# Sixteen instead of twelve pairs of projection tiles as block products, and the token-shift mixer's chunks refilled with six or seven tiles

## What is computed

```python
h = layer_norm(x)
u = h @ w_in                                   # 1024 x 14720: 115 tiles of 128 columns
u_gate, u_gla, u_rwkv, u_ssm = split(u)
o_gla  = gated_linear_attention(u_gla)         # chunked scan
o_rwkv = token_shift_mixer(u_rwkv)             # us = u + (u_previous - u) * mu, then a chunked scan
o_ssm  = ssd(silu(causal_conv(u_ssm)))         # four taps over time, then a chunked scan
merged = g0 * (o_gla @ gla_wo) + g1 * (o_rwkv @ rwkv_wo) + g2 * (o_ssm @ ssm_wo)
h = layer_norm(alpha * x + merged @ w_out)
h = layer_norm(alpha * h + moe(h))
```

## Time and profile before

| | us |
|---|---|
| median of 3 runs | 1493.3 (1489.31 to 1493.69) |
| the profiled execution | 1490.3 |
| its span | 1488.5 |
| PE busy | 1437.6 (97%) |
| DVE, ACT, POOL busy | 724.7 (49%), 418.2 (28%), 205.4 (14%) |

### The profile page before, as it was taken

How to read it: one execution, slowest core, us unless ns; L and a number is a source line. 1 busy time by engine, 2 the same in 40 slices (tenths; PEclk the granted TensorE clock), 3 DMA queues, 4 the chain that set the end, 5 groups by cost and what they waited for, 6 DMA issues and landing times.

```text
span 1488.5 us, 32593 instructions
## 1 busy us (share of the span) xinstructions
PE 1437.6 (97%) x13647; PEld 1051.5 (71%) x13647; DVE 724.7 (49%) x1345; ACT 418.2 (28%) x965; POOL 205.4 (14%) x171
## 2 busy tenths in 40 slices
PE   7999999999999999999999999999999999999995
PEld 6997666777776777777668986776575767676751
DVE  7445787875735777734547654522212121121228
ACT  2335434343223544435432211111111111111111
POOL 3771113122010000020022000000101000010000
PEclk9999999999999999999999999999999999999998
DMA  8888466363345444664576638599999999999984
GB/s 281 186 162 172 152 159 182 111 212 96 110 119 160 115 117 119 204 184 131 161 262 183 215 139 359 198 385 401 420 427 427 426 429 429 425 428 429 429 342 202
DMA packets 157042, 375.38 MB, mean 252 GB/s; under 512 B 101724, under 2 KB 110316, under 8 KB 139232
## 3 DMA queue, kind: packets, MB, share of 16 engines
q1 hardware_dynamic: 140928, 345.78, 65.8%
q0 software_dynamic: 6576, 16.48, 3.2%
q10 hardware_dynamic: 9392, 11.06, 2.2%
HBM read 327.14 MB, written 51.95 MB: 255 GB/s over the span
## 4 chain that ended last, share of the span: by engine, by line
PE 79%; DVE 9%; DMA 5%; DVEq 2%; issue 2%; ACT 1%; ACTq 1%; SPq 0%; POOLq 0%
PE PS L698 21%; PE PS L1250 14%; PE PS L1217 7%; PE PS L1269 6%; PE PS L1096 6%; PE PS L715 6%; DVE region L1730 4%; PE PS L780 3%; PE PS L1222 2%; PE PS L1138 2%; DVE region L1737 2%; DMA region<-projected 2%; PE PS L788 1%; PE PS L1233 1%; DMA region<-expert_rows 1%
## 5 line engine op out<-in xcount | busy, mean ns | idle before, releaser
L698 PE MATMUL PS<-h0T,region 128*128 128x320 f32 x1424 | 406.6, 438 | 1.0 <-issue 1.0
L1353 ACT ACTIVATE region<-PS 128x320 f32<-128x320 f32 (+7 forms) x408 | 154.5, 389 | 682.7 <-PE PS L698 233.1
L698 PEld LDWEIGHTS PS<-h0T,region 128*128 128x128 f32 x1424 | 264.0, 190 | 113.5 <-issue 12.1
L1250 PE MATMUL PS<-region 128*64 128x512 f32 x1024 | 228.8, 592 | 0.0
L1250 PEld LDWEIGHTS PS<-region 128*64 128x64 f32 x1024 | 124.4, 137 | 92.2 <-issue 32.0
L1730 DVE TENSOR_TENSOR region<-region 128x512 f32<-128x512 f32 (+10 forms) x230 | 154.3, 691 | 30.3 <-DMA region<-wo 6.5
L1353 ACT ACTIVATE region<-region 128x256 f32<-128x256 f32 (+11 forms) x229 | 99.4, 465 | 116.2 <-DVEq L2148 24.1
L1269 PE MATMUL PS<-region,history 128*64 128x512 f32 x512 | 119.7, 596 | 0.8 <-ACTq L1692 0.5
L1217 PEld LDWEIGHTS PS<-region,h 128*128 128x128 f32 x864 | 100.6, 192 | 22.3 <-issue 22.2
L1730 DVE TENSOR_TENSOR history<-region,PS 128x256 f32<-128x256 f32 x32 | 13.5, 421 | 196.5 <-ACTq L1687 196.4
L1217 PE MATMUL PS<-region,h 128*128 128x128 f32 x864 | 108.1, 278 | 0.3 <-issue 0.3
(11 more groups left out here) (239 smaller groups left out, 1594.8 us busy)
## 6 DMA issues: line engine op xcount, KB each, us to landing
region<-moe_w SPq DMA_DIRECT2D x64, 2048.0 KB, 17.9
region<-moe_w SPq DMA_DIRECT2D x64, 1024.0 KB, 15.6
region<-w_in SPq DMA_DIRECT2D x115, 512.0 KB, 5.7
region<-wo SPq DMA_DIRECT2D x32, 512.0 KB, 4.7
projected<-region ACTq DMA_DIRECT2D x64, 167.5 KB, 3.7
expert_rows<-region SPq DMA_DIRECT2D x20, 512.0 KB, 7.0
region<-expert_rows SPq DMA_DIRECT2D x5, 2048.0 KB, 15.2
region<-projected SPq DMA_DIRECT2D x10, 768.0 KB, 6.5
```

The costliest lines, as they stand in the source:

```text
L698: last = mm(PS[:, 6 + i % 2, 0:NTOK], WR[:, i, k, :], H0T[:, k, :], start=(k == 0), stop=(k == KT - 1))
L1250: last = mm(PS[tiles(i), 2, :], XE[:, k, tiles(i)], W13[r][i][:, k * 512:k * 512 + 512], start=(k == 0), stop=(k == KT - 1))
L1353: return nc.scalar.activation(out, in_, f, **kw)
```

## The change

**Order of the tiles.** `PRE` is 36: sixteen pairs are block products, and 32 tiles instead of 40 are left for the chunks. The list `FILLS` gives the chunks 6, 6, 6, 7 and 7 of them. A table `TILE` maps the place n to the feature: the 24 convolved features stand at the places `MIXED`, which are the first two tiles behind the pairs and the first four (chunks 0 to 2) or five (chunks 3 and 4) fills of each chunk. The four new pairs are `T_MISC` and tiles of the state-space gate. The first store of the mixer's last rows and their load are done at pair 11.

**Inside a chunk.** Round 1 is followed by half a tile (six fills) or a whole one (seven), round 2 by half a tile, round 3 by none, round 4 by half a tile, and where there are six fills the half tile behind round 5 is left out. DVE convolves behind round 0, behind round 2 (seven fills only), behind the `SAS` copy and twice behind the `YS` copy; the other places are gone.

**Other edits.** ACT copies the chunk edges and the history of a tile (two small ACTIVATEs) only where they are used. Counts of semaphores follow `PRE`. SP's code shown above has the same order as before; only the value waited for on `conv_stored` is written as a count over `MIXED`.

```diff
-PRE = 28
+PRE = 36
-HEAD_R, FILL = 4, 8
+HEAD_R = 4
+FILLS = (6, 6, 6, 7, 7)
+STARTS = [N_RW + sum(FILLS[:c]) for c in range(NCH)]
+MIXED = [PRE, PRE + 1, *(STARTS[c] + f for c in range(NCH) for f in range(4 if c < 3 else 5))]
+def mixed_until(n):
+    return sum(1 for m in MIXED if m < n and m % RING == n % RING)
...
             for i in range(RING):
-                sp.wait_ge(sem(f"conv_stored{i}"), 16 * (24 // RING))
+                sp.wait_ge(sem(f"conv_stored{i}"), 16 * mixed_until(NT + (i - NT) % RING))
...
@@ PE, rwkv
-                one = c + 1
+                one, seven, final = c + 1, FILLS[c] == 7, FILLS[c] - 1
-                    if r in (1, 2):
-                        fill(2 + r)
-                    if r == 3:
-                        fill(5, first)
+                    if r == 1:
+                        fill(3, range(KT) if seven else first)
+                    if r == 2:
+                        fill(4 if seven else 3, first if seven else second)
                     if r == 4:
-                        fill(5, second)
+                        fill(4, second if seven else first)
...
-                fill(6, first)
+                if seven:
+                    fill(5, first)
                 pe.wait_ge(sem("rw_tt"), one)
...
-                fill(6, second)
+                fill(5 if seven else 4, second)
...
@@ ACT, move and rwkv
-                a_(STG[:, i, 1:NPC, 0:HIST], src[:, 0:NPC - 1, L - HIST:L], ACT.Copy)
-                a_(STG[:, i, 0:NCH:NPC, 0:HIST], HISTS[:, n, :, :], ACT.Copy)
+                if mixed or n < T_MISC:
+                    a_(STG[:, i, 1:NPC, 0:HIST], src[:, 0:NPC - 1, L - HIST:L], ACT.Copy)
+                    a_(STG[:, i, 0:NCH:NPC, 0:HIST], HISTS[:, TILE[n], :, :], ACT.Copy)
...
-                    if r < 3:
-                        fill(2 + r)
+                    if r == 0:
+                        fill(2)
+                    if r == (1 if FILLS[c] == 7 else 2):
+                        fill(3)
...
@@ DVE, rwkv
                 if late:
-                    convolve(N_RW + c * FILL - 2)
                     late_variance(c - 1)
...
-                convolve(N_RW + c * FILL + 3)
+                convolve(STARTS[c] + (2 if FILLS[c] == 7 else 1))
...
-                for f in (4, 5):
-                    convolve(N_RW + c * FILL + f)
+                for f in (3, 4) if FILLS[c] == 7 else (2, 3):
+                    convolve(STARTS[c] + f)
```

More of the change, by code:

```diff
@@ L45 @@
 N_RW = PRE + HEAD_R
-N_S0 = N_RW + NCH * FILL
+STARTS = [N_RW + sum(FILLS[:c]) for c in range(NCH)]
+N_S0 = N_RW + sum(FILLS)
 N_SSM = N_S0 + HEAD_S
@@ L50, with _order @@
 assert N_GLA + NPC * FILL_G == NT and N_S0 >= T_GLA and N_G0 >= T_GATE
+FIRST_IN = 16 * (PRE // RING - PAIRS // 4)
+MIXED = [PRE, PRE + 1, *(STARTS[c] + f for c in range(NCH) for f in range(4 if c < 3 else 5))]
+assert len(MIXED) == T_Z - T_XBC
+def _order():
+    others = iter([*range(T_Z, NT)])
+    conv = iter(range(T_XBC, T_Z))
+    rw = [n if n < 16 else n + 8 if n < 18 else n - 2 for n in range(T_MISC)]
+    return [*rw, T_MISC, *(next(conv) if n in MIXED else next(others) for n in range(T_MISC + 1, NT))]
+TILE = _order()
+assert sorted(TILE) == list(range(NT)) and TILE[N_S0:] == list(range(N_S0, NT))
+def mixed_until(n):
+    return sum(1 for m in MIXED if m < n and m % RING == n % RING)
 V_MU, V_W0, V_A0, V_KK, V_KA, V_RK, V_LNG, V_LNB = 0, 26, 34, 42, 50, 58, 66, 74
@@ L452, in fill_weights @@
             def fill_weights(c, fs):
-                for f in fs:
-                    weights(c * (FILL // RING) + (N_RW + f) // RING, (N_RW + f) % RING)
+                for n in (STARTS[c] + f for f in fs):
+                    weights(n // RING, n % RING)
             def state_out(s):
@@ L470, in _ @@
                 chunk_rows(c + 1)
-                fill_weights(c, range(FILL))
+                fill_weights(c, range(FILLS[c]))
                 clear_rows(c)
@@ L474, in _ @@
             chunk_rows(NPC)
-            fill_weights(NPC - 1, range(FILL))
+            fill_weights(NPC - 1, range(FILLS[NPC - 1]))
             fill_weights(NPC, range(RING))
@@ L478, in _ @@
             sp.dma_start(SS, io['st_rwkv']).then_inc(sem("state_in"), 16)
-            fill_weights(NPC, range(RING, FILL))
+            fill_weights(NPC, range(RING, FILLS[NPC]))
             def conv_rows(c):
@@ L917, in rwkv @@
                     front_bonus(c + 1)
-                fill(7, range(KT) if ahead else first)
+                fill(final, range(KT) if ahead else first)
                 pe.wait_ge(sem("rw_copied"), c * 4 + 3)
@@ L923, in rwkv @@
                 else:
-                    fill(7, second)
+                    fill(final, second)
             for n in range(PRE, N_RW):
@@ L1383, in move @@
                 n = m * RING + i
-                mixed = isinstance(n, int) and T_XBC <= n < T_XBC + 24
+                mixed = n in MIXED
                 act.wait_ge(sem("tile_done"), n + 1)
@@ L1475, in fill @@
                 def fill(f):
-                    move(c * (FILL // RING) + (N_RW + f) // RING, (N_RW + f) % RING)
+                    n = STARTS[c] + f
+                    move(n // RING, n % RING)
                 one, w = c + 1, banks(0, 2, 8, 2, L)
@@ L1510, in rwkv @@
                     front_exp(c + 1)
-                fill(5)
-                fill(6)
-                for f in range(7, FILL):
+                for f in range(4, FILLS[c]):
                     fill(f)
@@ L1832, in quads @@
                 dve.wait_ge(sem("quad_kept"), 4 * p + 1)
+                for n in (RING + 2 * p, RING + 2 * p + 1):
+                    if n - RING >= T_MISC:
+                        dve.wait_ge(sem(f"store_done{n % RING}"), (n // RING + 1) * 16)
                 tt(quad_out(a, 0), kept(u, 0), Z, add)
@@ L1842, in paired_shift @@
             def paired_shift(n):
-                i, row = n % RING, head_row(n)
+                i, row = n % RING, TILE[n]
                 dve.wait_ge(sem("tile_moved"), n + 3)
@@ L1862, in convolve @@
             def convolve(n):
[L1864 to L1866 removed]
+                i, k = n % RING, TILE[n] - T_XBC
                 tap = lambda q: VEC[:, V_CW + 24 * q + k:V_CW + 24 * q + k + 1]
@@ L2024, in rwkv @@
                 dve.drain().then_inc(sem("rw_copied"), 1)
-            for n in range(PRE - 1, PRE + 1):
-                convolve(n)
+            convolve(PRE)
             dve.wait_ge(sem("rw_us0"), rows_in_at(0))
@@ L2662, in rwkv @@
                 pool.drain().then_inc(sem("rw_late"), 1)
-                for f in range(1 if late else 0, 6):
-                    store(N_RW + c * FILL + f)
+                for f in range(1 if late else 0, 5 if FILLS[c] == 7 else 4):
+                    store(STARTS[c] + f)
             def store(n):
-                if T_XBC <= n < T_XBC + 24:
-                    pool.wait_ge(sem("tile_mixed"), n)
-                    pool.dma_start(ut[n, :, :, HIST:CW], CV[:, n % RING]).then_inc(sem(f"conv_stored{n % RING}"), 16)
-            for n in range(PRE - 1, PRE + 2):
+                pool.wait_ge(sem("tile_mixed"), TILE[n])
+                pool.dma_start(ut[TILE[n], :, :, HIST:CW], CV[:, n % RING]).then_inc(sem(f"conv_stored{n % RING}"), 16)
+            for n in (PRE, PRE + 1):
                 store(n)
```

87 lines of the change are left out of this document (33 added, 54 removed).

## The result

The changed kernel takes 1516.7 us (median; 1516.2 to 1518.2) against 1491.7 us of the kernel before beside it (1489.3 to 1493.7). The ratio is 1.0175, with a 95% interval of 1.0162 to 1.0188, so 25 us slower, where I had forecast 1505. The profiled execution took 1518.2 us, with a span of 1516.3.

A forecast was written before the change was run, and what follows sets the result against it. PE was taken as the bound, busy nearly all of each stage. Terms led by +30.5 (pairs), -35.4 (tiles) and +10.5 (SP) summed to +12.7: 1503.0 us, 1506.0 on the median's level, called 1505, range 1495 to 1514.

The forecast's parts named there:

- A: The forecast itself: new waits in the chunks and SP's queue at their end, 1505 us (1498 to 1513), chance 0.64.
- rival E: DVE's lateness handed from chunk to chunk and rows slowest to land: +20 us, 1513 and above, chance 0.09.
- Waits before round 0: Chunks 0 to 2: convolutions ahead of round 0's copy are gone, so PE's waits shrink, -2.6 us.
- the front: Mixer's front: earlier pair stores and one ACTIVATE instead of five shorten PE's waits, -1.2 us.
- Round 1: PE waits 0.9 us for ACT's copy in round 2 of chunks 1 and 2 and round 3 of chunk 3, +2.7.
- Behind round 5: Chunks 0 to 2: without the half tile PE waits for DVE's TT and SAS copies, +6.3 us.
- Ends of the chunks: Chunk tails: DVE's 13.4 us of work against PE's 13.1 makes PE wait, +1.0 us (0 to 4).
- The end of chunk 4: Two convolutions behind the YS copy delay the squares that PE's variance needs, +2.4 us.
- SP behind chunk 4: Weights queued behind SP's wait on conv_stored come late, so PE waits +10.5 us (5.2 to 16.5).
- The clock behind it: PE's clock drops after the long wait for weights behind chunk 4, slowing the work that follows, +1.9 us.
- The two gaps of "issue": Unexplained PE gaps between round 5 and TT in chunks 0 and 1 mostly don't come again, -3.4 us.
- Eight tiles less: Chunks: eight fewer tiles at 4.43 us each save PE time if nothing waits, -35.4 us.

The follow-up runs named there:

- half tile as load: Changed kernel with next weights before SP's conv_stored wait and zero stores behind second tiles, plus unused half-tile matmuls in chunks 0 to 2: ratio 1.0024.
- the weights ahead: Changed kernel with SP issuing the weights of the four plain tiles behind chunk 4 before its wait on conv_stored: 1504.0 us, ratio 1.0085.

## Why the prediction was half right

The direction and the likeliest case (A: new waits in the chunks, SP's queue at their end) were right; the time was 12 us too low and outside the range. The number lies where rival E stood (1513 and above), but E's mechanism did not come: PE has no wait for DVE at the end of chunks 0 to 3, and SP's term was smaller than forecast. The range was also said to take in most of E, of which it held only the edge, 1513 to 1514. Step by step:

- *Four more pairs*, +30.5: measured +30.4 (122.13 for 16 pairs, 7.63 each).
- *Waits before round 0* and *the front*: as worked out; -0.9 came already ahead of the first pair, which I had not forecast.
- *Round 1* (+2.7): ACT's copy is waited for 0.60 in chunk 1 and 1.12 in chunk 3; in chunk 2 a gap of "issue" of 1.26 stands there instead. 1.7 in all, so the forecast was 1.0 too high.
- *Behind round 5* (+6.3): the waits of chunks 0 to 2 at `TT` and `SAS` are 0.70, 1.00, 1.01 and 1.06, 1.06, 1.18, together 6.0. The half tile as load shows that they are the price of the half that was taken out.
- *Ends of the chunks* (+1.0): no wait stands there in chunks 0 to 3, so 1.0 too high.
- *The end of chunk 4* (+2.4): 2.2. A wait of 1.0 for DVE in round 4 of chunk 4 (L1987), behind the convolution that now stands in round 2, was in no step.
- *SP behind chunk 4* (+10.5): 9.39, shown by the weights ahead. From POOL's store to SP's next load it took 4.6 us (4.8 forecast), the loads of the rows 3.0 (4.5), the weights 4.4 (4.0). *The clock behind it* (+1.9): the four tiles took 2.9 more, at a granted clock of 0.50 and then 0.92; with the wait gone they took 17.46.
- *The two gaps of "issue"* (-3.4) is the step that failed. I took them for something that stood where PE's code stood, and let them go with the order of the code. They grew from 5.0 to 9.0 us, and behind that of chunk 1 a half tile took 3.60 us for its four matmuls (eight records) instead of 2.42, at a granted clock of 0.50 from 264.7 to 268.1 us. That is +5.2 against -3.4, 8.6 us beside the forecast and the largest part of the miss. The runs show what they hang on: on the DMA traffic of the burst of zeros and the row load while PE is in the rounds. With SP's queue alone changed the 9.0 us fell to 4.6 and 3.4, and the two transfers cost most with one right behind the other. SP's order by tiles is the link: with six tiles instead of eight in a chunk, everything behind them in its queue comes two tiles earlier in the chunk. I had followed that queue for the weights, and not for these two.
- *The rest of the program*, +4.2 where I had 0. From the product with `wo` to the end the profiled executions take 745.1 us before and 749.0 after, and in the other profiles, with the same code there, between 743.8 and 749.2. The 3.9 is thus within what one execution differs from another there; the medians differ by 25.0, the spans by 27.8. The traces show where it lies: behind two waits of PE (2.60 and 2.18 us before, 2.87 and 3.71 after) the granted clock was 0.50 for 6.8 us in all before and for 13.7 after, so that the stretches with them took 8.80 and 9.53 us before (from 756.75 and 787.40) and 10.27 and 12.20 after (from 780.68 and 812.68), 4.1 more.

- *Eight tiles less* (-35.4) is in part too much. Apart from the tiles, PE is busy in chunks 0 to 3 for 91.8 us before and 96.2 after (the windows sum to 241.89 us of PE, 150.06 of them on L698; after, to 215.78 and 119.59 on L718). These 4.4 us go with the number of PE's gaps and waits. From the first scores of chunk 0 to those of chunk 4 this busy time is 91.0 us with 9 of them (the kernel before with its burst moved), 91.9 with 11 (before), 93.0 with 15 (its burst on the rounds) and 96.3 with 23 (after); the changed kernel with the half tiles back has 15 and 93.4. One profile lies well off this line (the weights ahead, 21 and 98.3, with the clock at 0.50 for 6.8 us there). A row shows how it comes about: 64 products behind round 0 of chunk 0 take 1.16 us in one piece before, and 1.14 + 0.34 when the gap of 0.98 cuts them. By these figures a gap costs about 0.3 us beyond its idle time, an estimate that no run tested by itself.

In sum 12.7 forecast, +8.6 for the gaps and the clock behind one, +4.4 for the busy time, +1.0 for L1987, -1.0 for round 1, -0.3 behind round 5, -1.0 for the ends of the chunks, -0.2 for the end of chunk 4, +1.0 for the clock behind chunk 4, +4.2 for the rest, -1.1 for SP, -0.9 at the start: 27.4 against the 27.8 measured.

|---|---|---|---|
| 194.59 | 195.96 | 196.94 | 2.35 |
| 207.62 | 208.33 | 210.26 | 2.64 |
| 212.07 | 214.18 | 214.69 | 2.62 |
| 261.37 | 262.33 | 264.50 | 3.13 |
| 268.36 | 270.59 | 271.08 | 2.72 |
| 316.55 | 317.50 | 318.76 | 2.21 |
| 322.06 | 324.77 | 325.12 | 3.06 |
| 328.26 | 329.77 | 330.75 | 2.49 |

In the profiles of all fifteen kernels here, each of the 79 gaps of "issue" between 160 and 450 us ends 2.2 to 3.7 us behind the start of such a packet. Of PE's 226 waits with a named cause, 59 do. So a gap is PE waiting for its next packet of instructions, and it ends when that has arrived. In the longest one (bursts moved a chunk later, 323.34 to 328.06) even the packet's start, at 325.20, lies in the gap. That SP's transfers make the packets late is shown by the edits of SP's queue; by which way they do so, and why the gaps are twice as long in one chunk as in another, stays open.

## What to carry to other kernels

When a change makes a loop's body shorter, go through everything that is queued in that loop on each queue, bulk transfers with no deadline of their own above all, and see what it falls on now. A large store with no hurry is better placed away from dense small matmuls and from other bulk transfers; moving it so, and nothing else, made the kernel before 0.4% faster. When PE shows gaps that no semaphore explains, compare them with the packets of the instruction queue. And work that fills a wait for a chain of copies on another engine costs nothing where it is, so moving it elsewhere pays its full price: here eight tiles, 35 us, were taken out of the chunks for 30.4 us of pairs, and the chunks got only 16 us shorter, in part because of the gaps.

## What the runs showed of the hardware

- PE's gaps with no semaphore behind them are waits for its instructions: all 79 in 15 profiles end 2.2 to 3.7 us behind the start of a 16 KB packet of the instruction queue.
- They grow with the other DMA traffic. A burst of stores and a load directly behind one another (15 such places; share of the DMA engines 0.84 to 1.06 in the windows of 20 us that were read) came with 1.7 to 5.8 us of gaps, the two with SP's wait between them with 0 to 3.0, either of them with nothing next to it with 0 to 2.4 us.
- Granted clock behind waits: in the window with the idle 9.39 us it is 0.50, in the next 20 us 0.92; after a wait of 2.21 us four records of 128x256 took 2.07 us in one profile and 1.13 in another. The row of 24 products behind a wait of 0.9 to 3.8 us took from 3.50 to 6.32 us in the profiles, with no clear order by the wait.
- DMA stores from SP hardly hold up what is queued behind them in the chunks: with bursts of 3.5 MB ahead of four (changed kernel) or six (kernel before) of a chunk's loads of weights no wait for `w_in` came in the chunks.
